# Alternating the 512-column and the 256-column matmuls of a unit, tile by tile

## What is computed

```
# block 1
h = rmsnorm(x); proj = h @ w_in              # attention inputs, and three 256-wide inputs of a short convolution
y = group_rmsnorm(concat(attention_a, attention_b, B * conv3(C * x_c)))
x = x + y @ w_out
x = x + (silu(h @ w_gate) * (h @ w_up)) @ w_down          # 1024 -> 2816 -> 1024
# block 2
h = rms_norm(x); z_a, q, k, v, gates = split(h @ w_in_2)
merged = sigmoid(g0) * (y_a @ w_branch_a) + sigmoid(g1) * (y_b @ w_branch_b)
x = x + merged @ w_out_2
up = h2 @ w_up_2; a, val = up[:2816], up[2816:]
x = rms_norm(x + (gelu(conv3(a)) * val) @ w_down_2)
```

## Time and profile before

| | |
|---|---|
| median of three runs | 689.58 us |
| the profiled execution: its time | 689.52 us |
| its span, first to last instruction | 687.8 us |
| outside the span | 1.7 us |
| TensorE matmuls (PE) | 680.8 us busy, 3784 instructions |
| TensorE weight loads (PEld) | 586.9 us, 3784 instructions |
| VectorE / ScalarE / GpSimd | 482.7 / 416.9 / 91.2 us |

### The profile page before, as it was taken

The page is one execution under the profiler, slowest core; times in us unless marked ns, Lnnn a source line. Parts: engine busy times, 40 slices in busy tenths (PEclk is TensorE's granted clock), DMA queues, the critical chain, the costliest instruction groups (busy, mean ns, idle before and its releaser), DMA issues.

```text
span 687.8 us, 9420 instructions
## 1 busy us (share of the span) xinstructions
PE 680.8 (99%) x3784; PEld 586.9 (85%) x3784; DVE 482.7 (70%) x730; ACT 416.9 (61%) x706; POOL 91.2 (13%) x173
## 2 busy tenths in 40 slices
PE   9999999999999999999999999999999999999996
PEld 8888888888888888888888988888888888888885
DVE  6878796767666666667455767777868877777774
ACT  7787775755555555556555856665577755555553
POOL 3122020778200000012710000000000000000001
PEclk9999999999999999999999999999999999999999
DMA  9936534737555555536434336555453655555401
GB/s 343 386 133 230 199 122 155 280 126 244 184 187 192 202 196 197 189 131 218 177 148 154 123 123 213 197 191 179 160 212 135 228 201 184 183 187 187 178 1 61
DMA packets 19484, 126.13 MB, mean 183 GB/s; under 512 B 2416, under 2 KB 2544, under 8 KB 5232
## 3 DMA queue, kind: packets, MB, share of 16 engines
q1 hardware_dynamic: 19296, 125.34, 50.3%
q10 hardware_dynamic: 144, 0.20, 0.1%
HBM read 124.48 MB, written 1.05 MB: 183 GB/s over the span
## 4 chain that ended last, share of the span: by engine, by line
PE 99%; DVE 0%; issue 0%; ACT 0%; POOLq 0%; POOL 0%; ACTq 0%
PE bank L435 96%; PE bank L443 3%; DVE xres L1438 0%; POOLq L2121 0%; DVE last L1438 0%; ACT last L996 0%; ACT junk L993 0%; POOL ss L1932 0%; DVE ones L1465 0%; ACTq L145 0%
## 5 line engine op out<-in xcount | busy, mean ns | idle before, releaser
L1438 DVE TENSOR_TENSOR wlo<-raw,whi 128x1024 fp32r<-128x1024 f32 x222 | 270.5, 1230 | 61.5 <-ACT whi L996 58.1
L996 ACT ACTIVATE whi<-raw 128x1024 fp32r<-128x1024 f32 x222 | 230.4, 1052 | 5.8 <-PE bank L435 3.9
L435 PE MATMUL bank<-xb,whi 128*128 128x512 f32 x496 | 124.1, 392 | 0.0
L435 PE MATMUL bank<-xa,whi 128*128 128x512 f32 x432 | 108.2, 392 | 0.0
L435 PEld LDWEIGHTS bank<-xb,whi 128*128 128x128 f32 x496 | 90.4, 188 | 17.2
L435 PE MATMUL bank<-whi,xb 128*128 128x512 f32 (+1 forms) x352 | 96.2, 355 | 0.0
L435 PEld LDWEIGHTS bank<-xa,whi 128*128 128x128 f32 x432 | 78.9, 188 | 15.5
L435 PEld LDWEIGHTS bank<-xb,wlo 128*128 128x128 f32 x496 | 67.7, 190 | 4.9
L435 PEld LDWEIGHTS bank<-whi,xb 128*128 128x128 f32 x352 | 62.4, 190 | 9.0
L435 PE MATMUL bank<-whi,hh 128*128 128x512 f32 (+1 forms) x180 | 69.7, 387 | 0.0
L435 PE MATMUL bank<-wlo,hh 128*128 128x512 f32 (+1 forms) x180 | 69.6, 387 | 0.0
(11 more groups left out here) (246 smaller groups left out, 796.9 us busy)
## 6 DMA issues: line engine op xcount, KB each, us to landing
raw<-in_w_dram SPq DMA_DIRECT2D x109, 1024.0 KB, 4.8
first<-in_first_dram SPq DMA_DIRECT2D x8, 388.0 KB, 5.5
raw<-in_w_dram SPq DMA_DIRECT2D x4, 512.0 KB, 8.7
bias<-in_bias_dram SPq DMA_DIRECT2D x1, 1024.0 KB, 9.4
xres<-in_x_dram SPq DMA_DIRECT2D x1, 1024.0 KB, 8.1
gain<-in_ffn_norm_w_dram SPq DMA_DIRECT2D x1, 512.0 KB, 8.9
gain<-in_mix_norm_g_dram SPq DMA_DIRECT2D x1, 512.0 KB, 9.6
gain<-in_ffn_norm_g_dram SPq DMA_DIRECT2D x1, 512.0 KB, 5.0
```

Source lines behind the costliest of these rows:

```text
L435: return e.matmul(o, l, r, start=start, stop=stop)
L996: return e.activation(o, i, ACT.Copy, **options)
L1438: return e.tensor_tensor(out=o, in0=a, in1=b, op=op)
```

## The change

In a feature unit the two loops become one: for each tile k the 512-column matmul with w_hi is followed at once by the 256-column matmul with w_lo. In the branch units likewise, each tile in its own bank. The number of instructions, their operands, the waits ahead of a unit and the last matmul of a unit (a 256-column one, which counts up "free") stay as they are. Only the order of the 16 matmuls and their 16 weight loads is new.

```diff
             h, l = whi[u % NH], wlo[u % NH]
             for k in range(KT):
                 mm(pb[bank][:, :], h[:, k * 128:k * 128 + 128], flat(x[:, k, :, :]), k == 0, False)
-            for k in range(KT):
                 m = mm(pb[bank][:, 0:256], l[:, k * 128:k * 128 + 128], x[:, k, 0, :], False, k == KT - 1)
             return m
...
                     mm(pb[2 + b][:, :], h[:, k * 128:k * 128 + 128], flat(xa[:, k, :, :]), k in (0, 6), False)
-                for k in range(KT):
-                    m = mm(pb[2 + k // 6][:, 0:256], l[:, k * 128:k * 128 + 128], xa[:, k, 0, :], False, k in (5, 7))
+                    m = mm(pb[2 + b][:, 0:256], l[:, k * 128:k * 128 + 128], xa[:, k, 0, :], False, k in (5, 7))
                 m.then_inc(*pe.done("free", u))
```

## The result

| | before | after |
|---|---|---|
| median of five runs | 689.58 us | 693.38 us |
| lowest and highest | 689.10, 689.82 | 693.21, 693.95 |
| profiled execution: its time, its span | 689.52, 687.8 | 693.35, 691.6 |

The changed kernel is slower: the ratio is 1.0059, 95% interval 1.0048 to 1.0071, which is +3.8 us. The forecast was 691.3, which is +1.7 us, with a range of 686.8 to 695.0.

The account below looks back on a forecast made before the run. TensorE's matmuls, 99% busy at full clock, were taken as the bound. Span 687.8 + 1.7 around it + 0.8 for pairs + 0.8 for unit ends = 691.2 us (691.3 against the median), range 686.8 to 695.0.

Parts of the forecast that it names:

- the likeliest case: Alternating pairs in feature units at 0.350 us against 0.349, plus 0.8 us at unit ends: 691.3 us, chance 0.30.
- rival C: Alternating pairs stay disturbed for good: 0.233 + 0.120 = 0.353 us each, 694.3 us in total, chance 0.27.
- The bound: TensorE matmuls busy 99% at full clock, one 1.1 us wait; the change acts only through what neighbouring matmuls cost.
- A second wait: Another TensorE wait in the list beside the 1.1 us one at the start would show something outside the argument.
- The 512-column term: A 512-column matmul behind one 256-column matmul takes 0.233 us, bounds 0.227 and 0.236.
- The 256-column term: A 256-column matmul behind a lone 512-column one takes 0.117 us, the middle between 0.113 undisturbed and 0.120.
- The pair: One 512-column plus one 256-column matmul takes 0.350 us against 0.349 now; over 928 pairs +0.8 us.
- The ends: Where an alternating unit is followed by a stretch of 512-column matmuls, 0.020 us is paid 42 times: +0.8 us.
- Rival B: Half restored: short matmul undisturbed at 0.113, 512-column one at 0.233, pair 0.346 to 0.347 us; 688.1 us, chance 0.18.
- Rival D: Order of the matmuls is of no account, the sum of parts stays: 689.6 us, chance 0.10.
- Rival A: Weight loads better hidden, both sizes undisturbed: 0.340 us a pair, -8.5 us, 681.1 us, chance 0.15.

## Why the prediction held, point by point

The range held, but the likeliest case did not: its own range was 690.2 to 692.3 and its change +1.7 us, and 693.38 and +3.8 were measured. The range held because it was drawn wide enough to take in most of rival C, whose price for a pair came true. The direction is in part luck. The trace has two patterns for the alternation, and at the 0.3467 a pair of the short one, all 928 pairs would take some 2.6 us less than before (an estimate, 0.0028 below the mean of 0.3495 that 324.30 us make). Nothing in the rows of the prediction says which pattern would come.

**The bound** held: the clock stayed full and the change acts through neighbours alone. A second wait, which I had named as a sign against my working, did turn up, but it is the one of 0.4 us ahead of all feature units, and all that is not a pair takes 0.15 us less than before.

**The 512-column term** was mis-sized. I took 0.233, the first one behind a run of short ones, and wrote 0.236 as its upper end. It measured 232, 240 and 236 ns in turn, 0.236 in the mean. This term is the step that failed: a lone short neighbour costs the next 512-column matmul as much as it had seemed to cost only the second one behind a run.

**The 256-column term** held: 0.117 taken, 118, 120 and 114 measured, 0.117 in the mean. The reason that I gave, a state between undisturbed and fully disturbed, is not what the trace shows; it is one value after another in a fixed round.

**The pair** is therefore 0.3533 and not 0.350, and the term 928 x 0.9 ns should have been 928 x 4.2 ns = 3.9 us. That is the price of rival C, by another split than C had (0.233 + 0.120). C's own term was added up wrongly: 0.353 against 0.349 makes 3.6 to 3.7 us and not 3.9, so its time should have been about 694.1. The 0.47 for a slower kernel is a small slip as well, since C and "a bit over half" of the forecast case make some 0.43. With 0.27 rival C had the second-largest chance; the likeliest case, by 0.03, was the wrong one.

**The ends** were counted too high. I set 42 x 0.020 = 0.8. In the traces a couple in front of a down unit goes from 5.559 to 5.640, +81 ns, of which 16 x 4.2 = 67 are the pairs: 14 ns to an end, 0.6 us. I had let the saving of the first pair cancel at 7 ns; it is 13, the whole of 0.353 - 0.340.

**What I did not have**: 88 of the 928 pairs run in a short pattern at about 0.347, 0.6 us less. Sum: 3.9 + 0.6 - 0.6 = 3.9, and +3.86 measured over the pairs.

**Rival B** had the price of the short pattern, 0.3465, which only those 88 pairs have. **Rival D** fell: the same parts in another order took 328.16 instead of 324.30.

**Rival A** fell in the changed kernel, whose pairs are at 0.353, but half of its reasoning came true elsewhere: half loads in the short runs bring most of them to 113 ns, so the stream alone does not set the 0.120 of a run. What I held against it, that slow 512-column matmuls follow a run, turned out to be the stronger evidence. The Trainium skill (TensorE: Matmul & The Clock Gate, section LDWEIGHTS) gives a load as its number of columns over 1.2 GHz, by which 64 columns fewer make an estimated 53 ns less. The trace agrees (134 against 188 ns of duration, 54 ns less). But the widths from 272 to 448 columns show that the disturbance does not come from a load that fails to fit.

**Shown**: that neighbours of another size cost 10 to 13 ns a pair at 256, 272, 320 and 448 columns; that it is gone or halved when the stationary operand has 64 columns (0.340 with such loads under the short one, 0.347 with them under the long one); that neither the PSUM columns nor the room for the load decides; that the way in picks between fixed patterns. **Open**: whether it is the full load that disturbs, as I think, or the number of PSUM partitions written, since the halved loads came together with half as many partitions and I did not separate them; what in TensorE is behind it; and why uninterrupted runs of 512 columns are free of it.

## What to carry to other kernels

When TensorE is bound and never waits, read the distances between matmul starts by neighbourhood, not by size: the same 512-column matmul was at 227, 232, 236 or 241 ns. If short matmuls have to be mixed with full-width ones, do not alternate them one by one: eight and eight, or two and two, cost 0.348 to 0.349 a pair here, one and one 0.353. A number taken from the edge of a run is not the number of a pattern that repeats the edge, so put both ends of such a term into the range.

## What the runs showed that I had not expected

The starts settle into fixed rounds, repeated to within 1 ns unit after unit, and there is more than one for the same order (three pairs in 1.060 us, two pairs in 0.693). Sixteen columns more in a short matmul, 7 ns of streaming, cost 7.4 us over the changed kernel (700.78 against 693.38) where the columns alone make 928 x 0.007 = 6.6. Of this the pairs themselves took 6.1 and the down units behind them 0.027 more each. And two waits of TensorE of 2.75 and 2.15 us cost 3.3 us on top of themselves, since eight of the sixteen matmuls behind each ran at the lower clock: 5.49 us long the first time instead of 3.82.
